# Two blocks in one kernel: state-space outputs made feature-first, two heads side by side; first attention's scores from split bfloat16 operands

## The reference, cut to what matters

```python
# first block, attention: 8 heads of 64, one shared key and value head
logits = einsum('bqhd,bqkd->bqhk', qb, k_sel) * attn_scale       # over the chosen keys

# second block, state-space part: 16 heads of 64 features, 2 groups of 8 heads, 8 chunks of 128 positions
xg    = x * dt[..., None]
a_cs  = cumsum(adt)                                              # per head, inside a chunk
decay = exp(segsum(adt))                                         # [l, s] per head, lower triangle
cb    = einsum('bclgn,bcsgn->bcgls', cc, bc)
y_diag = einsum('bcgjls,bcsgjp->bclgjp', cb * decay, xg)
states = einsum('bcsgn,bcsgjp->bcgjpn', bc, xg * decay_to_end)   # h = h * chunk_decay + states
y_off  = einsum('bclgn,bcgjpn->bclgjp', cc, prev) * exp(a_cs)
y      = y_diag + y_off + d_skip * x
y_ssm  = rms_norm(y * silu(z_ssm), ssm_norm_g)                   # then y_ssm @ w_out[1024:]
```

## Time and profile before

| what | value |
|---|---|
| median of 3 runs | 1814.01 us (1813.96 to 1815.15) |
| the profiled execution | 1812.38 us, its span 1810.6 us |
| PE busy | 1755.1 us, 97% of the span |
| DVE, ACT, POOL busy | 1176.9, 761.0, 794.4 us |
| granted TensorE clock | 0.998 of full speed |
| first attention | about 575 to 745 us |
| 16 items of the state-space part | 1042.8 to 1180.6 us |
| turns with four units between | 1191 to 1221 us |

### The profile page before, as it was taken

One profiled execution on the slowest core, in us unless ns is written; L12 is line 12 of the kernel. 1 busy time (PEld: TensorE's weight loads), 2 busy tenths in 40 slices (PEclk: granted clock), 3 DMA queues, 4 the chain that ended last, 5 costly groups with the idle time before them and its releaser, 6 DMA issues.

```text
span 1810.6 us, 28433 instructions
## 1 busy us (share of the span) xinstructions
PE 1755.1 (97%) x10946; PEld 915.8 (51%) x11118; DVE 1176.9 (65%) x2282; ACT 761.0 (42%) x1432; POOL 794.4 (44%) x744
## 2 busy tenths in 40 slices
PE   8999999999999999999999999999999999999998
PEld 5534455454444555544545555554455555555543
DVE  5668799999998777431545686847155555545647
ACT  4533652453213667312422467742144444444510
POOL 0520453462832314678611311118566555762560
PEclk9999999999999999999999999999999999999999
DMA  9010111211421012222312203202311111111332
GB/s 397 19 58 34 49 47 65 88 62 72 178 96 53 24 59 100 117 100 87 151 47 72 71 35 117 82 21 86 104 36 54 57 33 40 45 53 57 138 128 93
DMA packets 41606, 145.94 MB, mean 81 GB/s; under 512 B 6432, under 2 KB 12832, under 8 KB 37248
## 3 DMA queue, kind: packets, MB, share of 16 engines
q1 hardware_dynamic: 37248, 120.56, 18.2%
q0 software_dynamic: 4224, 23.56, 3.3%
HBM read 117.82 MB, written 23.13 MB: 78 GB/s over the span
## 4 chain that ended last, share of the span: by engine, by line
PE 77%; DVE 13%; ACT 3%; DMA 3%; issue 2%; POOL 1%; SPq 0%; DVEq 0%; ACTq 0%; POOLq 0%
PE ps L1299 39%; PE ps L1772 14%; PE ps L1293 4%; DVE small L2514 3%; DVE arena L2266 3%; PE ps L1349 2%; PE ps L1434 2%; PE ps L1791 2%; PE ps L1375 2%; PE ps L1336 2%; DMA hT<-in_mods 1%; PE ps L1408 1%; PE ps L1578 1%; PE ps L1731 1%; PE ps L1416 1%
## 5 line engine op out<-in xcount | busy, mean ns | idle before, releaser
L1299 PE MATMUL ps<-hT,W 128*128 128x512 bf16 x2196 | 491.5, 379 | 12.2 <-ACT arena L1875 4.2
L1299 PEld LDWEIGHTS ps<-hT,W 128*128 128x128 bf16 x2256 | 217.3, 98 | 274.5 <-issue 11.8
L920 POOL TENSOR_TENSOR W<-W 128x512 bf16<-128x512 f32 x118 | 134.8, 1180 | 267.4 <-DMA W<-in_loads 201.1
L1299 PE MATMUL ps<-W,arena 128*128 128x512 bf16 x916 | 206.9, 381 | 1.2
L1947 ACT ACTIVATE arena<-arena,small 128x128 f32<-128x128 f32 (+9 forms) x192 | 123.0, 641 | 147.1 <-DVE small L2343 118.7
L1954 ACT ACTIVATE arena<-arena,small 128x128 f32<-128x128 f32 (+9 forms) x192 | 114.0, 641 | 119.0 <-DVE small L2355 98.3
L1299 PEld LDWEIGHTS ps<-W,arena 128*128 128x128 bf16 x936 | 91.2, 97 | 112.1
L2514 DVE TENSOR_SCALAR_CACHE_REDUCE small<-arena,small 128x640 bf16<-128x640 f32 (+1 forms) x124 | 126.5, 1077 | 1.1
L1299 PE MATMUL ps<-arena,W 128*128 128x512 bf16 x569 | 124.5, 379 | 1.1 <-POOL arena L981 0.8
L2982 DVE TENSOR_TENSOR arena<-ps,arena 128x512 f32<-128x512 f32 x70 | 51.0, 728 | 101.6 <-PE ps L1772 101.6
L1772 PE MATMUL ps<-arena,W 128*128 128x512 bf16 x470 | 109.7, 379 | 1.2
(11 more groups left out here) (386 smaller groups left out, 3229.6 us busy)
## 6 DMA issues: line engine op xcount, KB each, us to landing
W<-in_loads SPq DMA_DIRECT2D x20, 2048.0 KB, 8.1
W<-in_groups SPq DMA_DIRECT2D x51, 256.0 KB, 3.9
W<-in_loads SPq DMA_DIRECT2D x5, 1792.0 KB, 7.0
gates_scratch<-arena SPq DMA_DIRECT2D x32, 256.0 KB, 2.0
arena<-gates_scratch POOLq DMA_DIRECT2D x2, 4096.0 KB, 13.6
arena<-sums_scratch SPq DMA_DIRECT2D x16, 512.0 KB, 3.8
W<-in_mods SPq DMA_DIRECT2D x2, 2048.0 KB, 16.9
hT<-in_mods SPq DMA_DIRECT2D x2, 2048.0 KB, 21.2
```

The source lines that it names most:

```text
L920: last = nc.gpsimd.tensor_tensor(low(v), v, high(v), ALU.subtract)
L1299: last = mm(o, left[:, :, a], moving, start=(k == 0 and (a, b) == PRODUCTS[0]), stop=(k == steps - 1 and (a, b) == PRODUCTS[-1]))
```

## The change

Four edits in one.

1. **State-space outputs with features on partitions.** The weights are now the inputs (128x64 per head) and the moving operand is the decay matrix, 128 columns. The two heads of a pair write to partitions 0 to 63 and 64 to 127 of the same PSUM bank. The term y_off goes into the same sums: its weights are the state (128x64), its moving operand is C times exp(a_cs) per head, a tile `growth` of 128x1024. A second row load per item brings exp(a_cs), and POOL multiplies it by C. The skip term's inputs come back from DRAM (SP stores the eight feature tiles after the convolution, and loads 4x128 columns per item), and POOL multiplies them by the skip weights. `Z` is feature-first, so the gate units swap weights and moving operand, and their weights are no longer planar.
2. **Decays in place.** The decay rows are loaded into three buffers, and ACT and DVE work in the same buffer. A row for item m is loaded when PE has done item m-3.
3. **No turn.** `turn_tiles` is gone. POOL adds the squares of an item over its feature tiles, and eight products with ones sum them over partitions. ACT and DVE make the high and low parts of `mixS` straight from `Z`: eight of the 16 pieces in items 12 to 15, eight after. `pair0`'s split moves into items 6 to 9 of POOL's loop, and `woS0`'s split comes after its last squares.
4. **First attention's scores.** Keys and queries are split by POOL (3 instructions of 128x1024 for the keys, 4 for the queries), and each float32 product becomes three bfloat16 products.

```diff
@@ PE, scores of the first attention
-                        for x in range(2):
-                            last = mm(ps[:, 2 + 2 * x + a // BANK, 0:e - a], q_of(items[n], halves[x]),
-                                      k_of(items[n], halves[x])[:, a:e], start=True, stop=True)
+                        for qp, kp in PRODUCTS:
+                            for x in range(2):
+                                last = mm(ps[:, 2 + 2 * x + a // BANK, 0:e - a], q_of(items[n], halves[x])[:, :, qp],
+                                          k_of(items[n], halves[x])[:, a:e, kp], start=((qp, kp) == PRODUCTS[0]),
+                                          stop=((qp, kp) == PRODUCTS[-1]))
@@ PE, an item of the state-space part
-                for h in range(8):
-                    last = mm(ps[:, 5, h * DH:(h + 1) * DH], decay[m % 2][:, h, :], xg[m % 2][:, h * DH:(h + 1) * DH],
-                              start=True, stop=True)
-                if c > 0:
-                    last = mm(ps[:, 6, :], CTf[:, g, c * P:(c + 1) * P], hst[:, g * 512:g * 512 + 512], start=True,
-                              stop=True)
+                if c:
+                    pe.wait_ge(s_scaled, growth_scaled(m))
+                for q in range(4):
+                    for x in range(2):
+                        h = 2 * q + x
+                        last = mm(ps[halves[x], 5, q * P:(q + 1) * P], xg[m % 2][:, h * DH:(h + 1) * DH], decay[m % 3][:, h, :],
+                                  start=True, stop=(c == 0))
+                    if c:
+                        for x in range(2):
+                            h = 2 * q + x
+                            last = mm(ps[halves[x], 5, q * P:(q + 1) * P], hst[:, h * DH:(h + 1) * DH], growth[m % 2][:, h, :],
+                                      start=False, stop=True)
@@ PE, after the items
-            pe.wait_ge(s_yo, 16)
...
-            turn_tiles(Z, s_gated, s_nrm["ssm"][4], s_nrm["ssm"][5], between_turns)
+            pe.wait_ge(s_sqadd, 16)
+            for t in range(NT):
+                last = mm(ps[:, 4, t:t + 1], y2_sum[:, t * P:(t + 1) * P], ones[:, 0:1], start=True, stop=True)
+            last.then_inc(s_nrm["ssm"][4], 1)
+            for u in range(FIRST["pair0"] + PAIR_AHEAD, unit_end("pair0")):
+                unit(u)
@@ SP
             def sums_row(m):
+                if m >= 3:
+                    sp.wait_ge(s_yd, m - 2)
+                nc.sync.dma_start(decay[m % 3].rearrange("p h l -> p (h l)"), row_of(0, m)).then_inc(s_rows[m % 3], 16)
+            def state_rows(m):
                 c, g = chunk_of(m)
                 if m >= 2:
-                    sp.wait_ge(s_dec, m - 1)
+                    sp.wait_ge(s_yd, m - 1)
+                    sp.wait_ge(s_scaled, growth_scaled(m - 2))
+                if c:
+                    nc.sync.dma_start(growth[m % 2].rearrange("p h l -> p (h l)"), row_of(1, m)).then_inc(s_es[m % 2], 16)
+                if m >= 2:
+                    sp.wait_ge(s_gated, m - 1)
+                nc.sync.dma_start(skip[m % 2], inputs_dram[:, 4 * g:4 * g + 4, c * P:(c + 1) * P]).then_inc(s_es[m % 2], 16)
@@ POOL, per item
+            def state_scaled(m):
+                c, g = chunk_of(m)
+                pool.wait_ge(s_es[m % 2], state_loads(m))
+                if c:
+                    t = growth[m % 2]
+                    mult(t, t, CTf[:, g, c * P:(c + 1) * P].unsqueeze(1).to_broadcast([P, 8, P])).then_inc(s_scaled, 1)
+                mult(skip[m % 2], skip[m % 2], par("dskip2")[:, 4 * g:4 * g + 4].unsqueeze(2).to_broadcast([P, 4, P]))\
+                    .then_inc(s_scaled, 1)
...
+            for m in range(1, 16):
+                if m + 1 < 16:
+                    state_scaled(m + 1)
+                squares_added(m - 1)
+                if 6 <= m < 10:
+                    split("pair0", (2 * m - 12, 2 * m - 10))
@@ ACT, items
             for m in range(16):
                 if m + 2 < 16:
                     decays(m + 2)
+                if m >= 1:
+                    gated_squares(m - 1)
                 if m + 3 < 16:
                     differences(m + 3)
-                if m >= 1:
-                    gated_squares(m - 1)
+                if m >= 12:
+                    mix_high(2 * (m - 12))
+                    mix_high(2 * (m - 12) + 1)
                 if m + 1 < 16:
-                    evac(FIRST["zs0"] + AHEAD + m + 1)
+                    evac(FIRST["zs0"] + AHEAD + m)
@@ DVE, after PE's products of an item
+                y_made = V.tensor_tensor(y, y, ps[:, 5, :].rearrange("p (q l) -> p q l", q=4), ALU.add)
...
+                if m >= 12:
+                    mix_low(2 * (m - 12))
+                    mix_low(2 * (m - 12) + 1)
```

More of the change, by code:

```diff
@@ L88 @@
 LOADS = weight_plan()
-PLANAR = ("out0", "zs0", "zs1", "woS0", "woS1", "woA0", "woA1")
+PLANAR = ("out0", "woS0", "woS1", "woA0", "woA1")
 SPARE_CHUNK = 16
@@ L244, in unit_plan @@
     units[a:a + 16] = OUT_ORDER
+    for name in ("zs0", "zs1"):
+        a = first[name]
+        units[a:a + 8] = [(name, i) for i in Z_ORDER]
     a = first["xbc0"]
@@ L491, in layer_kernel @@
         ss = little(8)
-        ssp = little(2 * NT)
         rs = little(8)
@@ L650, in chunk_of, with state_loads, growth_scaled @@
             return m % NT, m // NT
+        def state_loads(m):
+            return 16 * sum(1 + (k % NT > 0) for k in range(m % 2, m + 1, 2))
+        def growth_scaled(m):
+            return sum(1 + (k % NT > 0) for k in range(m)) + 1
         def loads_done(n):
@@ L1021, in _ @@
             split("ao")
+            pool.wait_ge(s_qback, 16)
+            for f in range(4):
+                v = qT1[:, f, :]
+                nc.gpsimd.tensor_tensor(low(v), v, high(v), ALU.subtract).then_inc(s_parts, 1)
+            pool.wait_ge(s_parts, FIRST_SPLITS)
             split("gb1")
@@ L1306, in units @@
                     unit(u)
-            def turn_tiles(src, rows_made, made, read, between):
-                for n in range(16):
-                    k, half = turned(n)
-                    if n == 0:
-                        pe.wait_ge(rows_made, 16)
-                    if n >= 4:
-                        pe.wait_ge(read, n - 3)
-                    for j in range(4):
-                        last = nc.tensor.transpose(ps[:, 4 + n % 4, j * P:(j + 1) * P],
-                                                   src[:, 4 * half + j, k * P:(k + 1) * P], ident)
-                    last.then_inc(made, 1)
-                    between(n)
             halves = (slice(0, DH), slice(DH, P))
@@ L1717, in _ @@
             chunk_scores(0)
-            unit(ahead + AHEAD)
+            unit(ahead + 2)
+            unit(ahead + 3)
             pe.wait_ge(s_xs, 10)
@@ L1901, in evac @@
                 elif name in ("zs0", "zs1"):
-                    last = A(Z[:, i, int(name[2]) * 512:int(name[2]) * 512 + 512], bank, ACT.Silu)
+                    last = A(Z[:, 4 * int(name[2]) + i // 2, half], bank, ACT.Silu)
                 elif name[:4] == "pair":
@@ L2828, in masked_products, with mix_low @@
                 dve.wait_ge(s_cbm, m + 1)
-                d = decay[m % 2]
+                d = decay[m % 3]
                 mult(d, d, cbm[m % 2].unsqueeze(1).to_broadcast([P, 8, CHUNK])).then_inc(s_mt, 1)
+            def mix_low(n):
+                f, half = MIX_ORDER[n]
+                span = slice(half * 512, half * 512 + 512)
+                dve.wait_ge(s_mixh, n + 1)
+                v = mixS[:, f, span]
+                V.scalar_tensor_tensor(low(v), Z[:, f, span], par("ssmg")[:, f:f + 1], high(v), ALU.mult, ALU.subtract)\
+                    .then_inc(s_nrm["ssm"][5], 1)
             scaled_inputs(0)
```

276 lines of the change are left out of this document (151 added, 125 removed).

## The result

| | before | after |
|---|---|---|
| median of 4 runs each, same chip | 1813.99 us (1811.53 to 1815.15) | 1795.12 us (1793.61 to 1795.55) |
| profiled execution, span | 1812.38, 1810.6 us | 1793.61, 1791.8 us |

The ratio is 0.9899, with a 95% interval of 0.9886 to 0.9912: faster by 18.9 us. The forecast of 1787 asked for 27, so 8.1 us are missing, and the change of the span, 18.8 us, is missing the same.

What follows compares the result with a forecast made beforehand. PE, busy for 97% of the span, was taken as the bound. Terms of -11.8, -8.2, -8.5, -2.4, +1 and +3 sum to -26.9 us, giving 1787 for the median; own range 1779 to 1794, wider range 1776 to 1804.

Steps and rivals of the forecast that it cites:

- Part 1: State-space items on PE: narrow products by decays and growth shorten an item to 8.16 us; -11.8 us.
- Part 2: Stretch from item 15 to `woS0`: turns and their waits go, products with ones add 1.8; -8.2 us.
- Part 3: First attention's scores as three bfloat16 products: -8.5 us, bounds -4 and -10.6, some falling into waits for DVE.
- Part 4: Items: PE's 2.37 us wait for ACT's evacuation goes, as rows land sooner after their issue; -2.4 us.
- Part 5a: Growth rows for the items arrive in time, with a small delay at the start; +1 us, bounds 0 and +6.
- Part 5b: From item 12, `mixS` pieces behind a late row delay DVE, so PE waits before item 14's products; +3 us.
- Part 5d: Items: work moved from DVE to POOL costs nothing, since some of each instruction's time can overlap.
- rival 1: DVE and POOL in turn set the items' pace: about 1802 us, chance 0.18.
- Rivals 2 to 4: Attention scores give nothing (1795, 0.09); two heads not side by side (1810, 0.04); growth-row round trip slows items (1829, 0.07).
- rival 2: First attention's new scores give nothing, because DVE's chain between scores and transposes is late next: 1795 us, chance 0.09.

Runs made afterwards that it cites:

- e7: e2 with B's product moved into the middle of the narrow products, instead of behind them: 1797.58 us, ratio 0.9915.
- e4: The changed kernel with B's product ahead of the products by decays and growth in each item: 1794.83 us, ratio 0.9898.
- e3: The changed kernel with the first attention's scores in float32 again, without GpSimd's splits for them: 1801.44 us, ratio 0.9934.
- e8: e2 with all 16 `mixS` pieces after item 15 and ACT's evacuations of three units set between the high pieces: 1785.77 us, ratio 0.9848.
- e9: e8 with `woS0`'s load ahead of the rows of items 14 and 15 again, as in the changed kernel: 1786.17 us, ratio 0.9847.
- e2: The changed kernel with item 15's decay row and item 14's state rows requested before `woS0`'s load: 1789.54 us, ratio 0.9871.
- e6: e2 with GpSimd making half of the growth product twice: 1802.22 us, ratio 0.9940.
- e5: e2 with GpSimd leaving out nearly all of the growth product and of the sums of squares: 1787.36 us, ratio 0.9856.
- e1_mix_last: The changed kernel with all 16 `mixS` pieces made after item 15, none in items 12 to 15: 1792.24 us, ratio 0.9885.

## Why the prediction was right, and where it was not

The forecast's sign, its main terms and its range of 1776 to 1804 held. The time came out 8.1 us above it, 1.1 us above the narrower range of 1779 to 1794 that I gave the forecast alone. By its steps:

- **Part 1, products.** The two heads run side by side, and decays and growth together take 1.90 us, as said. What failed is the item's sum: 8.35 for 8.16. I took the start of the narrow products as paid once, and did not price the return to products on the whole array. Each item changes from 128 to 64 columns and back; in the records the first narrow product comes 0.1 late and B's second record 0.1 late. All 16 items have both changes: 16 x 0.19 = 3.0 us. e7 shows that such a change costs, e4 that the order alone doesn't matter. The earlier trace rows held the same change, and I read from them only the length inside the narrow group. The Trainium skill, page "TensorEngine Tiling (Array Packing)", section "Key Properties", says that changing the tiling mode drains the engine: the rows agree in kind, and e7's 0.35 us for two changes is the size.
- **Part 2, the turns.** 27.4 us from item 15 to `woS0`, forecast 27.7; the products with ones take 1.70 from start to start (1.84 with their modelled end), forecast 1.8. `woS0`'s split was in time. Right for the new kernel, but I took the end of the window in the earlier trace rows, 1221.7, for the start of `woS0` in the old one. It starts at 1220.62, so the waits among the turns were 1.9 us and not 3, and the gain was put 1.1 too high.
- **Part 3, scores.** -8.5 forecast, within the bounds. The items began 1.6 us earlier (1041.23 against 1042.79) with one more unit of 5.2 us ahead of them, which makes 6.8; e3 puts it at 6.3. The scores themselves lost 10.8 us, all of the 10.6 that I had as the most. What I mis-sized is what falls into waits: PE's waits for ACT in the stretch grew from 4.7 to 7.7 us, and I had looked at waits for DVE. Off by 1.7.
- **Part 4, the wait that goes.** It went: no PE wait over 0.7 us in items 2 to 13. But it was worth 4.3 us and not 2.4, since the clock was at its lower level behind it. The forecast got 1.9 us less than it should have from this part, and that hid as much of the misses elsewhere.
- **Part 5a, growth rows.** +1 forecast; one wait of 0.66 us for GpSimd, before item 11. Right. It comes behind the four splits of `pair0`, not at the start as I had put it.
- **Part 5b, the interlock in item 12.** The mechanism was right link by link, the size wrong: +3 forecast, and 5.98 us of wait plus about 1.8 us of low clock measured (from the scores to B's product item 14 took 9.16 us, and 7.39 in e8: 1150.58 to 1157.97). I had let PE wait before item 14's products. But its small scores product comes first and waits for DVE's masking of the scores before, so the wait began 5 us sooner. The clock was not in my sum at all, here or in part 4. Nor were the 1.6 us by which GpSimd held up DVE's low pieces. This is the term that failed most, by almost 5 us: e9 without pieces in the items lost all of it, e2 two thirds.
- **Part 5d and rival 1.** The price was nothing, nearly as forecast, but the reason was wrong: I held that the two engines' instructions overlap in part, and they take turns. DVE loses at least 19 us in 100 by it. In the regular items it costs PE nothing, because PE's loop is 8.35 us and both queues fit in with their slack; at item 14, where that slack is gone, it makes 1.6 us of the wait in the changed kernel and the 2.33 us in e2. e6 shows how little is left: half a growth product more, about 1.04 us an item if it takes what e5's product of 512 columns takes alone, cost 12.7 us.
- **Rivals 2 to 4** fell: the scores gave most of their part, the heads run side by side, and rows landed in 4.4 us (median). The measured time is rival 2's number, 1795; e3, where giving up the new scores costs 6.3 us, rules out its mechanism.

The account: 3.0 (changes of array width), 4.9 (interlock and clock, 7.9 for 3), 1.7 (scores, 6.8 for 8.5) and 1.1 (the misread start of `woS0`) make 10.7 for the 8.1 missing. The old wait gave back 1.9 (4.3 for 2.4), growth rows 0.3, the stretch to `woS0` 0.3, which leaves 8.2. So the miss is 8 us and not 10 only by luck: a gain that I had priced too low made up for part of the losses.

## What to carry to other kernels

Work that has slack, such as preparing the next stage's operand, must not be queued on two in-order engines behind a load that can be late: placed after the loop it cost nothing and gave 8 us, but then look for what is queued behind it there, since evacuations that stood behind it took the whole gain back. When you trace a wait forward, look for the first instruction of the waiting engine that needs the late queue, however small it is, and add what a low clock costs behind it: here 1.8 us behind a wait of 5.98 and as much behind one of 2.37. That holds for a wait that a change removes too. Packing two heads into the array's column halves pays by the length of the narrow group, so keep the group in one piece.

## What the runs showed of the hardware

- After PE had idled for 5.98 us (4.34 us in e1_mix_last) the granted clock stood at 0.50, the lower of its two levels, 1.2 GHz, and was back at 1.00 about 3.5 us after work began in the changed kernel; in e1 the 6 us from 1184 on still had 0.73 in the mean. That is about 1.8 us lost on top of a wait of 6. In the kernel before, a wait of 2.37 us was followed by 0.50 too, from 1103 to 1105, and by 1.00 from 1106 on, 1.8 us lost as well; after e2's wait of 2.33 us the clock stayed at 1.00. So a wait of that length may or may not bring the lower level.
- Two more changes between 128 and 64 columns of the array in an item cost 0.35 us (e7, float32 products); alternating between two kinds of narrow products cost nothing.
- DVE instructions with two inputs in SBUF and GpSimd's products take turns; in the pairs read here the later one ended its own time, less 0.15 us, after the earlier.
- A 512 KB broadcast row landed in 4.4 us (median), and in about 7.7 behind a 2 MB load issued 3 us before it.
